# Attention in a two-layer hybrid block: transposed tile in two halves, softmax sums from ones beside V, division on GpSimd per pair of heads, value products one unit later

## What is computed

```python
def one_block(qi):
    s = jnp.einsum('bqhgd,bshd->bhgqs', qi, k).astype(jnp.float32)
    p = jax.nn.softmax(s, axis=-1).astype(v.dtype)
    return jnp.einsum('bhgqs,bshd->bqhgd', p, v)
...
ya = attention(q, k, v) @ lp['w_attn_o']
yb = multiscale_pool(u_pool, lp['pool_w'], lp['pool_scale']) @ lp['w_pool_o']
yc = conformer_conv(u_conv, ...) @ lp['w_conv_o']      # a depthwise convolution of 31 taps inside
merged = g[..., 0, :] * ya + g[..., 1, :] * yb + g[..., 2, :] * yc
```

## Time and profile before

| what | value |
|---|---|
| median of three runs | 2191.34 us (2189.56 to 2195.04) |
| the profiled execution, its own time | 2191.78 us |
| its span, first to last instruction | 2190.0 us |
| busy: PE, DVE, ACT, POOL | 97%, 61%, 37%, 36% of the span |
| layer 0's attention, first scores to the next large product | 132.4 to 248.5 us |
| layer 1's attention | 1375.5 to 1472.1 us |

### The profile page before, as it was taken

The page is one execution under the profiler, slowest core; times in us unless marked ns, Lnnn a source line. Parts: engine busy times, 40 slices in busy tenths (PEclk is TensorE's granted clock), DMA queues, the critical chain, the costliest instruction groups (busy, mean ns, idle before and its releaser), DMA issues.

```text
span 2190.0 us, 28107 instructions
## 1 busy us (share of the span) xinstructions
PE 2124.9 (97%) x11340; PEld 1789.5 (82%) x11340; DVE 1329.9 (61%) x1809; ACT 804.8 (37%) x1189; POOL 787.1 (36%) x366
## 2 busy tenths in 40 slices
PE   9999999999999999999999999899999999999997
PEld 7877888888888888888888887778777877888885
DVE  7369899855873688847616785989854362111113
ACT  5457411233224522222212356662244353222223
POOL 3310123232435433323323365004344475444442
PEclk8999999999999999999999999999999999999998
DMA  7100012132453234533323313002232423322321
GB/s 274 58 30 1 25 57 64 34 121 92 142 164 108 73 128 126 183 116 126 106 78 115 93 66 111 20 1 82 86 93 82 143 79 97 96 94 90 96 87 67
DMA packets 63200, 202.62 MB, mean 93 GB/s; under 512 B 7136, under 2 KB 8416, under 8 KB 63072
## 3 DMA queue, kind: packets, MB, share of 16 engines
q1 hardware_dynamic: 58608, 191.56, 27.0%
q10 hardware_dynamic: 4464, 9.28, 1.2%
HBM read 195.17 MB, written 5.64 MB: 92 GB/s over the span
## 4 chain that ended last, share of the span: by engine, by line
PE 80%; DVE 15%; ACT 3%; issue 1%; DMA 1%; POOL 1%; ACTq 0%; DVEq 0%; POOLq 0%
PE ps L560 73%; DVE conv_acc L1716 3%; DVE ps L1716 2%; DVE unit_stats L1677 2%; PE ps L586 1%; DVE pt1l L1697 1%; DVE pt0l L1697 1%; DVE probs L1691 1%; PE ps L795 1%; PE ps L629 1%; PE ps L647 1%; PE ps L638 1%; PE ps L816 1%; PE ps L668 1%; DMA w_raw<-in_w 1%
## 5 line engine op out<-in xcount | busy, mean ns | idle before, releaser
L455 POOL TENSOR_TENSOR w_l<-w_raw,w_h 128x1024 fp32r<-128x1024 f32 (+3 forms) x296 | 677.3, 2293 | 1283.0 <-ACT w_h L954 1282.9
L560 PE MATMUL ps<-h_h,w_h 128*128 128x512 f32 (+1 forms) x1296 | 428.0, 370 | 8.4 <-ACT t L1234 4.2
L560 PE MATMUL ps<-h_l,w_h 128*128 128x512 f32 (+1 forms) x1296 | 425.2, 368 | 0.0
L560 PE MATMUL ps<-h_h,w_l 128*128 128x512 f32 (+1 forms) x1296 | 424.7, 368 | 0.0
L954 ACT ACTIVATE w_h<-w_raw 128x1024 fp32r<-128x1024 f32 (+3 forms) x296 | 277.5, 939 | 236.0 <-PE ps L560 148.7
L560 PEld LDWEIGHTS ps<-h_h,w_h 128*128 128x128 f32 x1296 | 243.3, 188 | 59.0 <-ACT t L1234 6.0
L560 PEld LDWEIGHTS ps<-h_h,w_l 128*128 128x128 f32 x1296 | 244.4, 189 | 44.0
L560 PEld LDWEIGHTS ps<-h_l,w_h 128*128 128x128 f32 x1296 | 243.9, 188 | 42.6 <-issue 1.2
L1547 DVE CUSTOM_DVE_ANT_0 ps<-ada_raw,c_row 128x1024 f32<-128x1024 f32 x160 | 271.0, 1694 | 10.5 <-DMA ada_raw<-in_ada 5.4
L560 PE MATMUL ps<-f_h,w_h 128*128 128x258 f32 (+1 forms) x672 | 173.1, 339 | 0.9 <-DVE t L1902 0.9
L560 PE MATMUL ps<-f_h,w_l 128*128 128x258 f32 (+1 forms) x672 | 173.5, 340 | 0.0
(11 more groups left out here) (256 smaller groups left out, 3220.9 us busy)
## 6 DMA issues: line engine op xcount, KB each, us to landing
w_raw<-in_w SPq DMA_DIRECT2D x216, 512.0 KB, 3.6
ada_raw<-in_ada SPq DMA_DIRECT2D x80, 512.0 KB, 3.7
w_raw<-in_w SPq DMA_DIRECT2D x56, 256.0 KB, 3.2
w_raw<-in_w SPq DMA_DIRECT2D x16, 384.0 KB, 3.1
ada_near<-in_ada SPq DMA_DIRECT2D x10, 512.0 KB, 10.2
ada_far<-in_ada SPq DMA_DIRECT2D x6, 512.0 KB, 14.8
x_again<-in_x ACTq DMA_DIRECT2D x8, 384.0 KB, 7.5
x_between<-x SPq DMA_DIRECT2D x8, 384.0 KB, 2.9
```

Source lines behind the costliest of these rows:

```text
L455: nc.gpsimd.tensor_tensor(wl[:, s % RING, 0:n], raw[:, s % RAW, 0:n], wh[:, s % RING, 0:n], ALU.subtract).then_inc(split, 1)
L560: ins = nc.tensor.matmul(at(out, c0, c1), w[:, s % RING, b * P:(b + 1) * P], m[:, kt, first + c0:first + c1], start=(kt == 0 and n == 0), ...
```

## The change

- The transposed tile `B` is used in two halves, one PSUM bank each (`turned`). Tr, C and L of a unit are done half by half, each half with semaphores of its own. C and L are then two instructions of 384 columns (256 in the context unit) each.
- `probs` stays undivided: the reciprocal and the multiplication of N are gone, and exp no longer writes its accumulator. `transposes` waits for E in their place. The row maximum goes to PSUM (`A[u % 2][:, 0:n]`).
- `vh` becomes two tiles of 128 columns, one for each key head: 64 columns of V's high part and 64 of ones. Two of the three value matmuls have 128 columns of weights, so rows 64 to 127 of the product hold the sum of the probabilities. O becomes two copies of 64x256: the sums to `ada_raw`, the product to `o_raw`.
- GpSimd divides, per pair of heads j (`divide_by_sums`): a power of minus one, three instructions of a Newton step, and the product, each on 128x768 in layer 0 and 128x512 in layer 1. Each waits for the one before (`chain`). They stand ahead of the split of slab `S_CONV + 5`.
- `value_steps` begins a unit later, and in TensorE's loop the value step stands ahead of the transposes.
- ACT's rounding and DVE's subtraction of the attention output are done for three pairs after the units; the fourth pair's come after the first tanh on ACT and after the first 11 taps on DVE.
- Around it: `v_second` shares memory with `t2`, so `q1` uses `t3`; v's high part is written by four ACT instructions.

```diff
@@ value_steps @@
-            for u in range(2, len(us) + 2):
-                if us[u - 2][3] == us[u - 2][4] - 1:
+            for u in range(3, len(us) + 3):
+                if us[u - 3][3] == us[u - 3][4] - 1:
...
+        def turned(unit, half):
+            n = KT // 2 - 1 if q_tiles(unit) == 1 else CTX // P
+            return psf[:, 2048 + LAT * half:2048 + LAT * half + n * P]
+        def o_sum(j):
+            return ada_raw[:, j % 2]
@@ gpsimd @@
+            def chain(ins, *name):
+                ins.then_inc(*pool_norm.up(*name))
+                pool.wait_ge(*pool_norm.ago())
+            def divide_by_sums(ly, lo, j):
+                last_b = max(b for h, _, _, _, _, b in units(ly) if h == 2 * j + 1)
+                pool.wait_ge(*seen("free", "pv", ly, last_b))
+                total, inverse = o_sum(j)[:, lo:T], (t1[:, lo:T] if j < BR - 1 else o_sum(j - 1)[:, lo:T])
+                chain(nc.gpsimd.tensor_tensor(inverse, total, minus_one[:, 0:1].to_broadcast([P, T - lo]), ALU.pow))
+                chain(nc.gpsimd.tensor_tensor(total, total, inverse, ALU.mult))
+                chain(nc.gpsimd.tensor_scalar(total, total, -1.0, 2.0, ALU.mult, ALU.add))
+                chain(nc.gpsimd.tensor_tensor(inverse, inverse, total, ALU.mult))
+                chain(nc.gpsimd.tensor_tensor(o_raw[:, j, lo:T], o_raw[:, j, lo:T], inverse, ALU.mult), "o", ly, j)
...
+                split_run(at_s, ly * SLABS + S_CONV + 1 + RING)
+                at_s = ly * SLABS + S_CONV + 1 + RING
+                pool.wait_ge(*seen("free", "cval", ly, 0))
+                for j in range(BR):
+                    divide_by_sums(ly, lo, j)
@@ tensor, transposes @@
-                    take("B", "pt", ly, u)
-                    pe.wait_ge(*seen("normed", ly, u))
+                    pe.wait_ge(*seen("free", "scores", ly, u))
+                    for half in range(2):
+                        take(("B", half), "pt", ly, u, half)
+                        for k in range(0, n, P):
...
@@ tensor, values @@
-                        for n, (v, p) in enumerate(((vh, ph), (vh, pl), (vl, ph))):
-                            ins = nc.tensor.matmul(ODs[b % 2][0:HD, 0:2 * P], v[:, k, d0:d0 + HD], p[:, k, :],
+                        nc.tensor.matmul(out, vh[h // 4][:, k, :], ph[:, k, :], start=(k == 0), stop=False)
+                        nc.tensor.matmul(out[0:HD], vl[:, k, d0:d0 + HD], ph[:, k, :], start=False, stop=False)
+                        ins = nc.tensor.matmul(out, vh[h // 4][:, k, :], pl[:, k, :], start=False,
...
-                    if 1 <= u <= len(us):
-                        transposes(u - 1)
                     for step in plan.get(u, ()):
                         values(*step)
+                    if 1 <= u <= len(us):
+                        transposes(u - 1)
@@ scalar, o_out @@
+                    if h % 2 == 0 and q0 == CTX and j >= 2:
+                        act.wait_ge(*seen("o", ly, j - 2))
+                    nc.scalar.activation(o_sum(j)[p:p + 64, q0:q0 + 2 * P], ODs[b % 2][HD:P, 0:2 * P],
@@ vector @@
-                        link(v.reciprocal(ust[:, 3, c:c + n], ust[:, 2, c:c + n]), dve_tmp)
-                            v.tensor_scalar(p_r, p_r, ust[:, 3, c + r:c + r + 1], None, ALU.mult).then_inc(
+                        for half in range(2):
+                            dve.wait_ge(*seen("pth", ly, u - 2, half))
...
```

More of the change, by code:

```diff
@@ L335, in value_steps @@
             todo, out = [], {}
-            for u in range(2, len(us) + 2):
-                if us[u - 2][3] == us[u - 2][4] - 1:
-                    parts = 1 if us[u - 2][2] == CTX else 2
-                    todo += [(u - 2, part, parts) for part in range(parts)]
-                n = 1 if u < len(us) + 1 else len(todo)
+            for u in range(3, len(us) + 3):
+                if us[u - 3][3] == us[u - 3][4] - 1:
+                    parts = 1 if us[u - 3][2] == CTX else 2
+                    todo += [(u - 3, part, parts) for part in range(parts)]
+                n = 1 if u < len(us) + 2 else len(todo)
                 out[u], todo = todo[:n], todo[n:]
@@ L808, in values @@
                             pe.wait_ge(*seen("tile", ly, "v"))
-                        pe.wait_ge(*seen("free", "pt", ly, u))
+                            pe.wait_ge(*seen("ones", ly))
+                    pe.wait_ge(*seen("free", "pt", ly, u, part if parts == 2 else 1))
                     ph, pl = pt(b)
@@ L823, in _ @@
                 plan = value_steps(us)
-                for u in range(len(us) + 2):
+                for u in range(len(us) + 3):
                     if u + 1 < len(us):
                         scores(u + 1)
+                    for step in plan.get(u, ()):
+                        values(*step)
                     if 1 <= u <= len(us):
                         transposes(u - 1)
-                    for step in plan.get(u, ()):
-                        values(*step)
                 for j in range(1, BR):
@@ L1115, in _ @@
                 act.wait_ge(*seen("vt", ly))
-                nc.scalar.activation(vh[:].rearrange("p a b -> p (a b)"), at(B, 0, T),
-                                     ACT.Copy).then_inc(*act_hi.up("vh", ly))
+                for g in range(KV):
+                    nc.scalar.activation(vh[g][:, :, 0:HD], group_columns(at(B, 0, T), g), ACT.Copy).then_inc(
+                        *(act_hi.up("vh", ly) if g else act_hi.up()))
+                for g in range(KV):
+                    ins = nc.scalar.activation(vh[g][:, :, HD:P], ones[:, 0:1].to_broadcast([P, 6, HD]), ACT.Copy)
+                    ins.then_inc(*(act_hi.up("ones", ly) if g else act_hi.up()))
                 result_of(s0 + S_Q + 1)
@@ L1644, in _ @@
                 dve.wait_ge(*seen("vh", ly))
-                v.tensor_tensor(vl[:].rearrange("p a b -> p (a b)"), at(B, 0, T),
-                                vh[:].rearrange("p a b -> p (a b)"), ALU.subtract).then_inc(
-                    *dve_lo.up("free", "vt", ly))
+                for g in range(KV):
+                    ins = v.tensor_tensor(vl[:, :, HD * g:HD * (g + 1)], group_columns(at(B, 0, T), g),
+                                          vh[g][:, :, 0:HD], ALU.subtract)
+                    ins.then_inc(*(dve_lo.up("free", "vt", ly) if g else dve_lo.up()))
                 noted[("tile", ly, "v")] = noted[("free", "vt", ly)]
@@ L1701, in _, with o_low @@
-                for j in range(BR):
+                        for half in range(2):
+                            dve.wait_ge(*seen("pth", ly, u - 2, half))
+                            v.tensor_tensor(key_rows(pl, us[u - 2], half), by_key(turned(us[u - 2], half)),
+                                            key_rows(ph, us[u - 2], half), ALU.subtract).then_inc(
+                                *dve_lo.up("free", "pt", ly, u - 2, half))
+                def o_low(j):
                     dve.wait_ge(*seen("oh", ly, j))
@@ L1704, in _ @@
                         *dve_lo.up("ol", ly, j))
+                for j in range(BR - 1):
+                    o_low(j)
                 a0 = 0 if lo == 0 else GL - HALF
```

94 lines of the change are left out of this document (48 added, 46 removed).

## The result

The changed kernel takes 2881.07 us in the median (2879.07 to 2884.74), the kernel before 2190.45 beside it (2187.14 to 2195.04): a ratio of 1.3154, interval 1.3133 to 1.3175. I had forecast 2177.6 and a range to 2196.

What follows compares the result with a forecast made beforehand. Bound: the ring over tile `B` (Tr, C, L) and DVE's own list, 2.77 us a unit. 2191.8 - 20.4 gained + 6.6 given back = 2178.0, less 0.4 for the median: 2177.6 us, range 2165 to 2196.

Steps and rivals of the forecast that it cites:

- P: Length of GpSimd's power on 768 columns, two thirds of it for 512; taken as 4 us, at least 1.84.
- the rival of the long power: GpSimd's division: slower from P = 12.3 us, 2197.5 us at 16; chance 0.25 of P over 8.3, 0.15 over 16.3.
- The formula beyond P = 18: GpSimd's first three divisions a layer, each 6.8 + P, cost nothing under a 24.7 us pair of heads while P is under 18.
- 2P/3 - 0.3: Layer 1, fourth pair's division after attention: the time in us that TensorE was forecast to stand waiting at its fourth product.
- P + 0.2: Layer 0, fourth pair's division after attention: the forecast delay in us, after what waits and slack absorb.
- given back: Forecast loss from the fourth pair's division in both layers: 6.6 us at P = 4, 3.0 at P = 1.84.
- The start of layer 1: Filling of layer 1's attention, 1375.5 to 1388.52 (13.0 us), with the same wait over tile `B`; given a gain of 1.0 us.
- The first rival: Both engines pack better, P is 1.84 us: unit at TensorE's 2.47 us, 24.8 gained, 2166.5 us; chance 0.18.
- The third rival: Attention units: the halves and their doubled waits on ACT eat the gain, unit stays at 2.7 us, 2187 us; chance 0.15.
- The ring through ACT: Attention: E of unit u+1 stands behind C of u-1 and O on ACT; 5.12 us for two units, 2.56 each.
- my floor: TensorE's least time for an attention unit: V to S 1.14, Tr to V 0.63, S 0.70, together 2.47 us.
- The price by the Trainium skill: GpSimd's power as branching code, about 12 cycles an element: 7.7 us for 768 columns, the sum then 7.7 us gained.

## Why the prediction was wrong

**The step that failed** is "I take P = 4 us, two products' length, nearest to the only rows there are". P is 122.6 us. I had written that no row bounds it from above, and then sized it by rows of another operation. The side on which it decides was worked out: the rival of the long power, with 12.3 us as the point. But it had a quarter of the chance, and its worked time stopped at 16 us and 2197.5, so the range ended at 2196 for an unknown without an upper end.

**The formula beyond P = 18** was only a remark, that "the first three pairs do not fit under attention either". That term is the larger one: 524 of 715 us. Its form was right: a pair lasts 24.7 us by my text and 24.8 in the trace, and what exceeds it is paid three times. With P = 122.6 and 81.9, its cover of 44.1 and 37.8 us and the fourth power on top, all taken from the runs, the given mechanism lands on the measured time.

**DVE behind the port.** I had it wait the whole power in both layers, by the rule of the Trainium skill, "SBUF — State Buffer", section "Who interferes with whom". In layer 0 the holds last to the power's end, with a gap behind the first 512 columns; in layer 1 nothing was held, and the kernel made for it shows no hold at 512 columns or fewer. The rule, a lock for a whole instruction, agrees with GpSimd's products and not with its powers. The time hardly depends on it: the fourth `o_l` must wait for the division in any case. The fourth powers cost 191.2 of the 202.0 us by which they exceed the products, where I had 2P/3 - 0.3 and P + 0.2, the whole. In layer 1, 8.6 us of taps run beside the power; by the traces of the two kernels layer 0 too takes some 8 us less than its power is longer, and what covers them there is not shown.

**The gain.** Forecast 20.4 us, less 3.0 given back at a product's price; measured 23.4 with the product for the power, and 21.6 with no division. The unit was right: forecast 2.56, measured 2.56 over the same 26 units, and a head of layer 0 is 12.37 in the mean of six in that kernel, for 12.34. Two other terms were off. The start of layer 1, which I gave 1.0 us, gains 3.7 (first scores to the sixth M, 13.9 before and 10.2 after: the units of the filling come 2.0 us apart, before they came 2.8 to 3.0); its end gains 2.5 for my 2.3. Layer 0 gains 12.7 for 11.6. And of the 3.0 given back nothing can be measured. The first rival, both engines packing better, needed a unit of 2.47 and was not met with V late; that its 2166.5 is only 1.8 us over what that kernel took is luck: it had the unit too short, and the gain of the start too small and the price of the division too high, which made up for it. The third rival, halves that gain nothing, fell: they are worth 0.43 us a unit.

**The ring through ACT.** I had charged V's new place with 1.14 us of a ring over two units of 5.12, in which the scores wait for E. Two units take 5.12 with V late, and that wait is in the trace. With V at its old place it does not bind, and the unit is TensorE's own: 2.42, where my floor was 2.47. So the step was right, but I never costed the move of V as an edit of its own, and it is a loss of some 9 us in the traces.

**The price by the Trainium skill.** By the Trainium skill, "GPSIMD Engine Reference", section "Elementwise — side-by-side cycle accounting", I had an estimate of 7.7 us for 768 columns. The trace shows 16 times that.

## What to carry to other kernels

An operation that appears in no row has no price: run it by itself behind the last store of the old kernel before it is put on a path, and until then leave its upper end open. On a serial engine, what a call exceeds the idle time before it is paid at every call, and a kernel with a cheap stand-in shows that idle time in its rows. When edits come together, take each back once: here the halves gave most, the lighter DVE less, and the move of V only cost. And measure a unit where the pipeline is full: an average that takes in its first units, which lack a part of the work, comes out too short.

## What the runs showed of the hardware

- GpSimd's elementwise power takes 0.16 us a column of 128 rows, 20.7 us at 128 and 122.6 at 768, with the exponent -1 as with 3.7. A scalar multiply-add on whole numbers, the same bits read as floats before and after, takes 0.83 us at 768.
- Beside a power of 768 or 640 columns DVE's instructions on two SBUF tensors, and then its copies, are held for some 82 us and again to the end; beside 512 or 256 they are not, where four products take 3.74 and 3.32 us for 2.8. The cause is not shown.
- DVE's reciprocal takes 4.95 us at 768 columns, 3.35 at 512 and 0.946 at 128, five times its product of 0.69 us at 512.
- After the long waits TensorE ran at its lower level: the slices of both attentions show a granted clock of 5 to 6 tenths, that is 1.2 of 2.4 GHz, where PE was busy 0 to 4 tenths; the first large products behind layer 1's third power come 0.43 us apart, later ones 0.23.
